# Gate and V of a GLA head in shared 512-column units, and the gate applied before the output is turned

## What is computed

```
proj = h @ w_in                      # q, k, v, g and a forget-gate code among its columns
log_a = log_sigmoid(code @ w2 + b) / 16
o = gla_chunked(q * DK**-0.5, k, v, log_a)        # chunked causal linear attention
o = rms_norm(o, gla_norm_w)                       # over the head's 256 channels, per token
o = o * silu(g)
```

## Time and profile before

| | |
|---|---|
| profiled execution, us | 1637.32 |
| its span, us | 1635.6 |
| median of three timed runs, us | 1637.13 |
| TensorE busy, us and share | 1601.0, 98% |
| VectorE busy | 1037.8, 63% |
| ScalarE busy | 843.1, 52% |
| POOL busy | 409.1, 25% |
| mean granted TensorE clock | 0.996 |

### The profile page before, as it was taken

One profiled execution on the slowest core, in us unless ns is written; L12 is line 12 of the kernel. 1 busy time (PEld: TensorE's weight loads), 2 busy tenths in 40 slices (PEclk: granted clock), 3 DMA queues, 4 the chain that ended last, 5 costly groups with the idle time before them and its releaser, 6 DMA issues. The chain is left out here.

```text
span 1635.6 us, 27436 instructions
## 1 busy us (share of the span) xinstructions
PE 1601.0 (98%) x9990; PEld 1383.0 (85%) x9990; DVE 1037.8 (63%) x1755; ACT 843.1 (52%) x1500; POOL 409.1 (25%) x450
## 2 busy tenths in 40 slices
PE   5999999999999999999999999999999999999998
PEld 4888888888888888898888888888888878888886
DVE  5545354465544544457777768877777854775987
ACT  5765564555444554465445556644545554334332
POOL 2301011102322222211222222233232220441424
PEclk9999999999999999999999999999999999999999
DMA  9523442265433633345222214322222336675886
GB/s 323 153 91 117 137 123 75 76 199 149 161 129 121 207 130 128 120 147 149 74 76 78 77 71 149 127 99 78 72 76 77 109 116 204 234 242 163 304 280 214
DMA packets 131502, 231.14 MB, mean 141 GB/s; under 512 B 9923, under 2 KB 81875, under 8 KB 126278
## 3 DMA queue, kind: packets, MB, share of 16 engines
q1 hardware_dynamic: 123910, 190.49, 36.4%
q10 hardware_dynamic: 6656, 39.06, 6.4%
q0 software_dynamic: 832, 0.22, 0.3%
HBM read 177.05 MB, written 52.70 MB: 140 GB/s over the span
## 5 line engine op out<-in xcount | busy, mean ns | idle before, releaser
L1170 PE MATMUL ps<-hl,w 128*128 128x512 f32 x1488 | 372.8, 399 | 0.5 <-ACT qk L620 0.5
L1170 PEld LDWEIGHTS ps<-hl,w 128*128 128x128 f32 x1488 | 273.9, 188 | 56.5 <-issue 1.7
L1904 PE MATMUL ps<-hl,w 128*128 128x256 f32 x2304 | 293.2, 287 | 1.7 <-ACT c_z L1635 1.6
L1904 PEld LDWEIGHTS ps<-hl,w 128*128 128x128 f32 x2304 | 280.5, 192 | 9.5 <-issue 9.2
L1176 PE MATMUL ps<-w,hl 128*128 128x256 f32 x1536 | 200.7, 287 | 0.0
L1176 PEld LDWEIGHTS ps<-w,hl 128*128 128x128 f32 x1536 | 190.4, 191 | 2.6 <-DVE w L865 0.4
L1770 DVE SCALAR_TENSOR_TENSOR c_acc<-c_before,conv_col,c_acc 128x256 f32<-128x256 f32 x288 | 159.2, 555 | 47.8 <-ACT c_acc L1630 41.0
L1908 PE MATMUL ps<-hl 128*128 128x512 f32 x768 | 178.6, 391 | 0.9 <-DVE hl L1739 0.9
L1908 PEld LDWEIGHTS ps<-hl 128*128 128x128 f32 x768 | 143.0, 188 | 30.2 <-DVE hl L1739 1.1
L2366 PE MATMUL ps<-w,hl 128*128 128x512 f32 x720 | 164.2, 389 | 0.0
L2366 PEld LDWEIGHTS ps<-w,hl 128*128 128x128 f32 x720 | 135.0, 188 | 28.3 <-issue 0.3
(11 more groups left out here) (257 smaller groups left out, 2639.9 us busy)
## 6 DMA issues: line engine op xcount, KB each, us to landing
x_sb<-h SPq DMA_DIRECT2D x52, 512.0 KB, 4.3
w_raw<-in_w_in SPq DMA_DIRECT2D x44, 512.0 KB, 5.3
c_ac<-step_sums ACTq DMA_DIRECT2D x16, 1024.0 KB, 4.6
d_a_raw<-mixed_in SPq DMA_DIRECT2D x29, 512.0 KB, 4.2
c_h_raw<-h SPq DMA_DIRECT2D x56, 256.0 KB, 2.8
d_a_raw<-mixed_in SPq DMA_DIRECT2D x11, 1024.0 KB, 6.0
w_sums<-late ACTq DMA_DIRECT2D x8, 1280.0 KB
w_raw<-w_sums SPq DMA_DIRECT2D x40, 256.0 KB, 3.9
```

The source lines that it names most:

```text
L1170: mm = pe.matmul(ps[:, PROJ + u % 2, :], w[:, u, k, a, :], hl[:, par, k, b, :], start=(k == 0 and i == 0), stop=(k == KT - 1 and i == 2))
L1904: mm = pe.matmul(ps[:, PROJ + u % 2, 0:B2], w[:, u, k, a, :], hl[:, par, k, b, :], start=(k == 0 and i == 0), stop=(k == KT - 1 and i == 2))
```

## The change

Gate and V of a head now lie side by side in one weight block `w_t` of 512 columns, with tokens stationary. Units 2 to 5 are the four token tiles: each is 24 matmuls of 512 columns, whose result has the gate in its first 256 columns and V in the others, and is evacuated in two copies. Step 0 keeps units of two tiles, gate ahead of V, in matmuls of 256 columns. A unit 2 to 5 needs all weights of its head (in step 0: those of its pair). The weights 2 to 5 can only be overwritten when the last unit of the head before is done: weight 2 is split in slot 11 of the last step, 3, 4 and 5 in slots 0, 1 and 2 of the next, and SyncE loads 4 and 5 at the start of that step.

The gate has tokens on the partitions, as the output has before it is turned. VectorE scales the output by rstd and multiplies it by the gate in one instruction, in slot i % 3 = 1 behind the state's update; this replaces ScalarE's scaled copy. After the turn ScalarE multiplies by the norm's weight into `y`, in slot i % 3 = 2. SiLU of step n-1 moves to slot 0 of step n. VectorE's order changes: the running sums ahead of the state's update, the code's low part and the products behind the multiply, the difference of `y` at the end of the step. The last step is rearranged alike.

```diff
-    UQ, UK, UG, UV = 0, 1, 2, 4
+    UQ, UK, UT = 0, 1, 2
...
-    W_SLOTS = tuple(2 * u + 3 for u in range(UV))
-    V_SLOTS = (1, 3)
-    LOW_SLOTS = (3, 6, 8, 9)
+    W_SLOTS = (3, 5, 3 * TB - 1)
+    T_SLOTS = (0, 1, 2)
...
-        w_v = w[:, UV:U].rearrange("p u k c n -> p (u k c n)").rearrange("p (k c n) -> p k c n", k=KT, c=2)
+        w_t = w[:, UT:U].rearrange("p u k c n -> p (u k c n)").rearrange("p (k c n) -> p k c n", k=KT, c=2)
...
+                    if s == 0 and n > 0:
+                        load_w(h, 4)
+                        load_w(h, 5)
...
-                            for u in ((2,), (3, 4), (5,), ())[q]:
+                            for u in ((), (2,), (3,), ())[q]:
                                 load_w(h + 1, u)
...
+                for u in (4, 5):
+                    load_w(GH, u)
...
-                wait(act, unit_done, (h * NB - 1) * U + (u + 1 if u < UV else U))
+                wait(act, unit_done, (h * NB - 1) * U + (u + 1 if u < UT else U))
...
+                    t = u - UT
+                    wait(act, gated_ready, (n - 1) * TB)
+                    act.activation(gz[:, n % 2, t, :], ps[:, PROJ + u % 2, 0:DV], ACT.Copy)
+                    wait(act, kv_done, (n - 1) * TB + t + 1)
+                    act.activation(v[:, t, :], ps[:, PROJ + u % 2, DV:2 * DV], ACT.Copy).then_inc(unit_out, 1)
...
             def silu_gate(n):
-                act.wait_ge(unit_out, n * U + UG + 2)
+                act.wait_ge(unit_out, n * U + U)
                 act.activation(gz[:, n % 2], gz[:, n % 2], ACT.Silu).then_inc(gsilu, 1)
-                act.preload_act_table_set("natural_log_exp_and_others")
+                if n < STEPS - 1:
+                    act.preload_act_table_set("natural_log_exp_and_others")
...
-                act.wait_ge(rstd_ready, m + 1)
-                wait(act, ot_done, m)
-                act.activation(o_n[:, :], ps[:, O, 0:DV], ACT.Copy, scale=rstd[:, :]).then_inc(on_ready, 1)
+            def weighted(r, t):
+                m = r * TB + t
+                act.wait_ge(ot_done, m + 1)
...
+                if t == 0:
+                    wait(act, y_stored, r * 48)
+                for f in range(2):
+                    last = act.activation(y[:, t, f, :], o_turned[:, f * P:(f + 1) * P], ACT.Copy,
+                                          scale=norm_col[:, f:f + 1])
+                last.then_inc(y_ready, 1)
...
+                    if n > 0 and i == 0:
+                        silu_gate(n - 1)
                     if n > 0 and i % 3 == 1:
-                        normed(n - 1, i // 3, m if i == 1 and 1 < m < NB else None)
+                        square(n - 1, i // 3)
+                    if n > 0 and i % 3 == 2:
+                        weighted(n - 1, i // 3)
...
-                    if i in V_SLOTS and s == 0 and n > 0:
-                        w_high(h, UV + V_SLOTS.index(i))
+                    if i in T_SLOTS and s == 0 and n > 0:
+                        w_high(h, 3 + T_SLOTS.index(i))
...
-                    if i == 7:
-                        silu_gate(n)
...
                         if i in (1, 2) and m > 1:
-                            for t in ((1, 2), (3,))[i - 1]:
-                                x_square(m, t)
+                            for t in range(2):
+                                x_square(m, (i - 1) * 2 + t)
...
-            for u in range(UV, U):
-                w_high(GH, u)
+            silu_gate(STEPS - 1)
+            w_high(GH, 3)
+            w_high(GH, 4)
...
             def gated(r, t):
                 m = r * TB + t
-                dve.wait_ge(ot_done, m + 1)
...
+                dve.wait_ge(rstd_ready, m + 1)
+                wait(dve, ot_done, m)
+                dve.scalar_tensor_tensor(out=o_n[:, :], in0=ps[:, O, 0:DV], scalar=rstd[:, :], in1=gz[:, r % 2, t, :],
+                                         op0=ALU.mult, op1=ALU.mult).then_inc(gated_ready, 1)
...
+                    if i == (6 if n == 0 else 4):
+                        gate_sums(n)
                     if i % 3 == 1 and n > 0:
                         update_state(n - 1, t)
+                        gated(n - 1, t)
+                    if 0 < n < NB and i == 1:
+                        code_low(n)
                     if i == 3 * TB - 2 and m >= NB:
                         products(n)
-                    if i % 3 == 2 and n > 0:
-                        gated(n - 1, t)
...
+            w_low(GH, 3)
             for t in range(TB - 1):
                 dve.wait_ge(kv_done, m + 1 + t // 2)
                 dve.wait_ge(state_ready, m + t)
...
+            for t in range(TB):
+                dve.scalar_tensor_tensor(out=o_all[:, t, :], in0=ps[:, LAST_O[t], 0:DV], scalar=x_rstd[:, t:t + 1],
+                                         in1=gz[:, (STEPS - 1) % 2, t, :], op0=ALU.mult,
+                                         op1=ALU.mult).then_inc(gated_ready, 1)
...
-                    pe.wait_ge(w_ready, h * U + (u + 1 if u < UV else U))
+                    pe.wait_ge(w_ready, h * U + (u + 1 if u < UT else U if n > 0 else (u // 2 + 1) * 2))
...
+                else:
+                    t = u - UT
+                    for k in range(half * KT // 2, (half + 1) * KT // 2):
+                        for i, (a, b) in enumerate(PASSES):
+                            mm = pe.matmul(ps[:, PROJ + u % 2, :], hl[:, par, k, a, t * P:(t + 1) * P], w_t[:, k, b, :],
                                            start=(k == 0 and i == 0), stop=(k == KT - 1 and i == 2))
...
             def turn(r, t):
                 m = r * TB + t
-                pe.wait_ge(on_ready, m + 1)
+                pe.wait_ge(gated_ready, m + 1)
```

## The result

The changed kernel takes 1670.2 us (median of four runs, 1667.5 to 1672.7) against 1638.2 for the kernel before on the same chip: ratio 1.0197, 95% interval 1.0185 to 1.0209. Forecast was 1659.1, in a range from 1646 to 1673. The direction and the kind of loss were right, the size was 11 us short.

What follows compares the result with a forecast made beforehand. TensorE was taken to bound attention, with no room. From 1637.3 us: - 7.8 + 0.5 + 5.4 + 1.7 + 7.9 + 9.0 + 2.1 + 3.0 = 1659.1 us, 1.4% slower, range 1646 to 1673.

Steps and rivals of the forecast that it cites:

- B: Step 0: first gate unit waits for VectorE's split of weight 3, 5.9 us, less 0.53 for x: +5.4 us.
- F: Last step: SiLU, weight splits and four multiplies on one engine delay the last turns, +3.0 us (+1.3 to +3.5).
- A: Merged units, steps 1 to 15: wide matmuls replace V's narrow ones, 7.8 us gained; step 0 loses 0.5.
- C: SiLU at the next step's head: turn and gate matmul late in steps 1 to 3, +7.9 us; ordinary steps free.
- D: New heads, steps 4, 8, 12: late weight splits and load of weight 5 delay half-unit 4, +9.0 us (5.7 to 11.1).
- E: VectorE forms products after the last tile's multiply: k_end's turn late in steps 9 to 14, +2.1 us (0 to 4.0).
- The clock: Step 0: after the long idle TensorE's clock falls to half for 3.3 us, +1.7 us (0 to 1.7).
- rival 2: Clock falls after each new wait, eight more places at 1.7 us: +13.6, 1672.7 us; chance 0.1.
- The margin of 0.36: Ordinary steps: the first tile's multiply ends 0.36 us before TensorE turns it, so moving SiLU costs nothing there.
- the first: Rival: not slower, wide matmuls at the recurrence's pace and waits at their least, 1634.6 us; chance 0.05.
- the third: Rival: each table switch costs its length again, 2.2 us in each of 15 steps, +33, 1692 us; chance 0.01.
- the fourth: Rival: waits in steps 1 to 3 and at heads hide better, at lower bounds, 1653 us, still slower; chance 0.14.

Runs made afterwards that it cites:

- e1: Changed kernel with each merged 512-column matmul of steps 1 to 15 split into two of 256 again: 1688.7 us.
- e4: Changed kernel with the split of weight 3 moved earlier in the opening on ScalarE and VectorE: 1663.8 us.
- e5: Changed kernel with 22 matmuls into an unread bank filling TensorE's wait for weight 3 in step 0: 1670.5 us.
- e9: Changed kernel with weight 3 split first at the new heads, steps 4, 8 and 12, on ScalarE ahead of K's copy and SiLU: 1672.2 us.
- e11: Changed kernel with the next head's load of weight 4 issued ahead of the store of y's difference: 1669.2 us.
- e12: e7 with SiLU first only in steps 1 to 3, weight 3 at heads as in e9, x's squares together, and weight 4's load as in e11: 1650.2 us.
- e3: Changed kernel with the gate's cumulative sums on VectorE moved back behind tile 1's state update and multiply: 1663.0 us.
- e2: Changed kernel with SiLU first in its step on ScalarE, ahead of K's copy and the code's low part: 1666.4 us.
- e7: Changed kernel with e3, e4, e8, the tail's splits behind its states and squares, and weight 3 ahead of SiLU at new heads: 1651.2 us.
- e8: e2 plus, in steps 1 to 3, K's copy ahead of the code's low part and the mask ahead of the code's sum: 1668.9 us.

## Why the prediction was right, and where not

The direction rested on one reading, that TensorE has no room in attention and that the change adds waits ahead of it. It held: TensorE's idle grew by 27.4 us, the very sum of terms B to F. That agreement is luck: a wait costs more than its idle, and some waits were not forecast while others came out smaller. The two traces, compared from the start of each half-unit of steps 1 to 15 to the start of the next (the half-unit in slot i and the piece of attention behind it), show where the time went, after less before:

| slots | us | term |
|---|---|---|
| 8 to 11, V before and merged after | -0.09 to -0.15 each, -6.5 in all (an old wait in step 8 left out) | A |
| 6 and 7, the gate before, merged after, as many wide matmuls | 0.04 or less each | A |
| 2, steps 1 to 3 | 2.73, 2.43, 2.44 | C |
| 2 and 3, steps 4, 8 and 12 | 2.27, 2.59, 3.74 | D |
| 0, steps 9 to 15 | 0.37, 0.10, 0.41, -0.19, 0.35, 0.36, 0.36 | E |
| 5, steps 3, 11 and 15 | 1.84, 1.85, 1.96 | none |
| 5, steps 9, 10, 13 and 14 | 0.50, 0.27, 0.56, 0.56 | none |

By terms:

- **A, the merged units: -7.3 forecast with step 0, about -6 found** (-6.5 and the 0.5 of step 0 as forecast). Each merged half-unit that was V's is some 0.1 us shorter, near the 0.13 that the prediction named as its sign; e1 gives the same the other way round. Where only the operands were exchanged, nothing changed. A step without waits shows the gain, one gate matmul to the next, before and then after:

```profile
320.77 0.48 PE L1229 MATMUL ps<-code,w 128*128 128x512 f32 x1
...
361.91 0.48 PE L1229 MATMUL ps<-code,w 128*128 128x512 f32 x1
```

```profile
338.92 0.47 PE L1250 MATMUL ps<-code,w 128*128 128x512 f32 x1
...
379.71 0.47 PE L1250 MATMUL ps<-code,w 128*128 128x512 f32 x1
```

41.14 became 40.79, 0.35 of the 0.52 a step. In step 13 waits hide it: 41.17 became 41.73, of which the traces show 0.50 as idle. The rest of what they cost is why only -1.8 was left above. The last matmul ahead of a wait takes 388 ns until the idle begins, where without a wait the next one starts after 231, and the turn behind the wait takes 165 ns to the next start instead of 108 (the profile models where a matmul ends); so tile 1's turn in step 11 idles 1.69 us and costs 1.85.
- **B, step 0: right.** 6.27 us at the place named, released by VectorE's split of weight 3; less the 0.47 and 0.53 of before, 5.3 for 5.4. e4 shows the cause. TensorE's rows for B, C (step 2, to set beside the earlier trace rows) and F, in order of time:

```profile
63.81 2.50 PE L1191 MATMUL ps<-w,hl 128*128 128x256 f32 x10 [6.27 <-DVE w L885]
...
160.06 0.44 PE L1242 MATMUL ps<-ident,o_n 128*128 128x128 f32 x2 [1.68 <-DVE o_n L944]
160.77 0.50 PE L1250 MATMUL ps<-code,w 128*128 128x512 f32 x1 [0.27 <-DVE code L866]
...
762.45 0.70 PE L1352 MATMUL ps<-late,q_all 128*128 128x256 f32 x2 [2.05 <-DVE late L1110]
```

- **The clock: the term that was too small.** +1.7 was taken behind step 0 alone; rival 2, a fall behind every wait, had a chance of 0.1. The truth lies between: falls at three places, 6.9 us, of which step 0's cost 2.1, and 2.5 more than before in the opening. The Trainium skill's rule of no idle gaps ("TensorE: Matmul & The Clock Gate", "Why this matters for your kernels") points the right way (61.20:68.00 at 0.50 here, and at 1.00 in e4 and e5).
- **C, steps 1 to 3: right in kind, too dear.** The turn and the gate matmul wait on VectorE as said (1.68 and 0.27 in step 2), 7.6 us in all by the table, 6.9 of it forecast. But the 1.0 for x did not come, and 1.3 us that the code had cost in slot 0 of steps 2 and 3 went: about 6 for 7.9. The margin of 0.36 in ordinary steps held: the first turn shows no idle in any of the nine and loses at most 0.18.
- **D, new heads: 8.6 for 9.0, with one link missing.** The load of weight 5 was named; e9, e11 and e12 show that of weight 4 to be about as late.
- **E, products: 2.1 forecast, 1.8 found.** The list of waits shows only 0.2, but the turn of k_end comes late in each of steps 9 to 15, with idle of 0.1 to 0.2 us. Over TensorE's matmuls and weight loads together the waits of this turn on dec grew from 1.5 us in 3 to 4.1 in 8. The weight load of step 13, before and then after:

```profile
645.34 0.14 PEld L1193 LDWEIGHTS ps<-ident,k_end 128*128 128x128 f32 x1
...
629.31 0.14 PEld L1214 LDWEIGHTS ps<-ident,k_end 128*128 128x128 f32 x1 [0.55 <-DVE dec L919]
```

- **F, the tail: 3.6 for 3.0 in waits**, though by another road: the states behind weight 3 (2.05) and c_acc behind the last y (1.22) rather than the last turns (0.69). With its fall of the clock, 6.7.
- **Not forecast at all: tile 1, 5.7 us in the last steps of three heads and 1.9 in steps 9, 10, 13 and 14.** The prediction gave each turn of an ordinary step the timing of tile 0. It did not follow the other line that the diff moves on VectorE, the sums ahead of the state and the multiply, at a slot where the weight splits stand too. e3 shows it: there slot 5 of these seven steps is back at the time of before.

Of the rivals, the first falls with A (252.1 ns where it needed 236 or less by the same count), the third with SiLU's loads, the fourth with the size of the result; the second was a third right (the two further falls cost 4.8 us of its 13.6).

So the mechanism held, and A, B, D, E and F came within 1.5 us each. Two things were missed: the clock, 8 us too low, and the moved line, 7.6 us. C was 2 too dear, and about 1 us is left unassigned. In medians the miss is 11, and that 1670.2 still lies within the range, near its upper end, is partly luck: the range did not know of the moved line.

## What to carry to other kernels

Where an engine has no room, a change that gives it better instructions but a shorter lead over its feeders is decided by the lead: list every line that the diff moves on every queue, and follow each at every slot where something else stands, not at one typical tile. Price a wait of the bound engine at a little more than its idle, and at a possible fall of the clock as well; compare start to start, because a list of idle times leaves out part of it. When a wait goes away in an experiment and the time doesn't, look at the granted clock before you drop the theory; and where undoing one link gains nothing, undo the second too.

## What was not expected of the hardware

- Waits of about 2 us sometimes bring TensorE's clock down and sometimes don't: 2.16 at 106 us did in after, 2.17 at 597 did not; 2.09 at 420 did in e2, 2.17 at 582 did not in e7. Even 1.68 did at 208 in e9, and not at 157. What decides is open. e7, with most waits under 1.3, had none; e8, with 3 us less idle than after, paid 3 us more for the clock.
- A tiny operation can more than double: POOL's power for rstd (128x1) took 1.40 us at 557.0 in after, beside VectorE's splits, where 0.57 is seen at 740.4 and 750.5 (spans on POOL are rough in the profile). It was not tried by itself.
